# The second layer of an MLP as seven products of quarter sums for eight

## The reference

```python
def sq_relu_mlp(h, w1, w2):
    return jnp.square(jax.nn.relu(h @ w1)) @ w2
# in the layer:  x = x + gt2 * sq_relu_mlp(modulate(rms_norm(x, norm2), sh2, sc2), w_mlp1, w_mlp2)
```

## Time and profile before

| | |
|---|---|
| median of 3 runs | 1731.2 us (1731.02 to 1736.15) |
| profiled execution | 1733.65 us, its span 1731.8 us |
| TensorE busy | 1690.8 us, 98% |
| VectorE, ScalarE, GpSimd busy | 1010.1, 831.4 and 702.9 us (58%, 48%, 41%) |
| MLP stage | from 1376 us to the end |
| mean granted TensorE clock | 0.999 |

### The profile page before, as it was taken

One profiled execution on the slowest core, in us unless ns is written; L12 is line 12 of the kernel. 1 busy time (PEld: TensorE's weight loads), 2 busy tenths in 40 slices (PEclk: granted clock), 3 DMA queues, 4 the chain that ended last, 5 costly groups with the idle time before them and its releaser, 6 DMA issues.

```text
span 1731.8 us, 24615 instructions
## 1 busy us (share of the span) xinstructions
PE 1690.8 (98%) x8729; PEld 1381.5 (80%) x8729; DVE 1010.1 (58%) x1568; ACT 831.4 (48%) x1464; POOL 702.9 (41%) x795
## 2 busy tenths in 40 slices
PE   8999999989999999999999999999999999999998
PEld 6878787768686667878888888888888888888887
DVE  5578785697457755376668657787534533222222
ACT  4465665776366654366642454565423331313131
POOL 2634445426451024411124332323245465655554
PEclk9999999999999999999999999999999999999999
DMA  7362624223321002211058521112233233333333
GB/s 223 112 184 86 188 90 122 87 84 87 87 90 39 13 25 76 62 35 28 25 188 269 150 61 38 50 42 57 61 97 90 81 86 97 98 97 97 97 98 109
DMA packets 217149, 160.54 MB, mean 93 GB/s; under 512 B 8333, under 2 KB 190614, under 8 KB 217046
## 3 DMA queue, kind: packets, MB, share of 16 engines
q1 hardware_dynamic: 201758, 125.50, 25.3%
q10 hardware_dynamic: 15288, 33.66, 5.8%
HBM read 156.98 MB, written 2.16 MB: 92 GB/s over the span
## 4 chain that ended last, share of the span: by engine, by line
PE 77%; DVE 7%; ACT 6%; issue 5%; POOL 2%; DMA 1%; ACTq 0%; DVEq 0%; SPq 0%; POOLq 0%
PE ps L666 17%; PE ps L670 17%; PE ps L667 17%; PE ps L3226 3%; PE ps L3229 3%; PE ps L3227 3%; PE ps L2276 2%; POOL wl L616 2%; DVE mod_late L2672 2%; PE ps L2258 2%; PE ps L1683 1%; PE ps L2265 1%; PE ps L2822 1%; DMA ada_late<-w_ada 1%; ACT wh L629 1%
## 5 line engine op out<-in xcount | busy, mean ns | idle before, releaser
L616 POOL TENSOR_TENSOR wl<-raw,wh 128x256 fp32r<-128x256 f32 (+1 forms) x775 | 679.9, 907 | 967.8 <-ACT wh L629 967.8
L666 PE MATMUL ps<-ah,wh 128*128 128x512 f32 (+1 forms) x1144 | 457.4, 400 | 5.1 <-DVE al L794 2.2
L670 PE MATMUL ps<-ah,wl 128*128 128x512 f32 (+1 forms) x1144 | 447.3, 391 | 0.2
L667 PE MATMUL ps<-al,wh 128*128 128x512 f32 (+1 forms) x1144 | 446.3, 390 | 0.0
L629 ACT ACTIVATE wh<-raw 128x1024 fp32r<-128x1024 f32 (+1 forms) x220 | 230.7, 1049 | 300.2 <-PE ps L670 141.7
L666 PEld LDWEIGHTS ps<-ah,wh 128*128 128x128 f32 (+1 forms) x1144 | 214.0, 187 | 58.2 <-issue 7.2
L670 PEld LDWEIGHTS ps<-ah,wl 128*128 128x128 f32 (+1 forms) x1144 | 213.7, 187 | 49.3 <-POOL wl L616 1.9
L667 PEld LDWEIGHTS ps<-al,wh 128*128 128x128 f32 (+1 forms) x1144 | 214.2, 187 | 44.0 <-issue 1.7
L666 PE MATMUL ps<-bh,wh 128*128 128x512 f32 (+1 forms) x332 | 133.3, 402 | 0.7 <-DVE bl L1518 0.5
L670 PE MATMUL ps<-bh,wl 128*128 128x512 f32 (+1 forms) x332 | 129.6, 390 | 0.1
L667 PE MATMUL ps<-bl,wh 128*128 128x512 f32 (+1 forms) x332 | 129.5, 390 | 0.0
(11 more groups left out here) (468 smaller groups left out, 2938.4 us busy)
## 6 DMA issues: line engine op xcount, KB each, us to landing
raw<-w_mlp SPq DMA_DIRECT2D x64, 512.0 KB, 3.9
raw<-w_in SPq DMA_DIRECT2D x52, 512.0 KB, 3.8
raw<-ssm_w_in SPq DMA_DIRECT2D x40, 512.0 KB, 4.1
ada_late<-w_ada ACTq DMA_DIRECT2D x16, 1024.0 KB, 7.9
ada_raw<-w_ada ACTq DMA_DIRECT2D x16, 512.0 KB, 4.7
cum_rows<-cum_saved ACTq DMA_DIRECT2D x16, 512.0 KB, 3.9
raw<-ssm_w_out SPq DMA_DIRECT2D x16, 512.0 KB, 3.3
raw<-mla_w_in SPq DMA_DIRECT2D x11, 512.0 KB, 4.0
```

The lines of the kernel that those rows point to most:

```text
L616: nc.gpsimd.tensor_tensor(wl[:, s, part], raw[:, s, part], wh[:, s, part].bitcast(F32), ALU.subtract).then_inc(lo_ready, LOW_PIECES * (par ...
L666: nc.tensor.matmul(dst, w_hi[k], x_hi[k], start=k == 0, stop=False)
L667: nc.tensor.matmul(dst, w_hi[k], x_lo[k], start=False, stop=False)
L670: ins = nc.tensor.matmul(dst, w_lo[k], x_hi[k], start=False, stop=k == n - 1)
```

## The change

The second layer is done as one level of Strassen's scheme (Winograd's form). The 1024 hidden columns of a trip and the 512 tokens are cut into halves, the weights of the trip (1024 x 1024) into four quarters of 512 x 512. Seven products of sums of quarters replace eight products of quarters.

- **Layout.** `hidden(n)` sends even units to chunks 0 to 3 and odd ones to chunks 4 to 7, so that units 2m and 2m + 1 hold the four pieces (128 x 256) that are summed.
- **Token sums.** After each odd unit VectorE forms four sums of 128 x 256 (`hidden_sums`); ScalarE makes high parts (`sums_high`) and VectorE low parts (`sums_low`).
- **Weights.** The second layer's weights no longer pass through `raw`. ScalarE's queue loads four quarters of 1 MB per trip (`load_quarter`). VectorE forms differences in place (`quarter_sum`, 1024 columns an operation), ScalarE makes high parts (`mid_high`), VectorE the low parts of five products (`mid_low`), GpSimd of two (P3 and P2), in pieces of 512 columns.
- **Products.** TensorE takes them in the order P1, P5, P6, P3, P7, P2, P4, each 24 matmuls: two halves of the weights, two token tiles, two chunks, three parts. Products that feed the same output follow each other into one bank where the scheme allows. P1 waits for all low parts but the last.
- **Output.** VectorE adds the banks to an accumulator `acc` over all four trips; the gate is applied once, in the last trip.

```diff
-        ("mlp", 4, [full] * 16),
+        ("mlp", 4, [full] * 8),
...
+        MID = ("P1", "P5", "P6", "P3", "P7", "P2", "P4")
+        MID_BANKS = ((2, 3), (4, 5), (2, 3), (4, 5), (2, 3), (6, 7), (2, 3))
+        MID_SIDE = (3, 5)
...
 # TensorE
+            def product(i, r):
+                first, goes_on = isinstance(i, int) and i == 0, r not in MID_BEGINS
+                for u in range(2):
+                    vh, vl = mid_slot(r, u)
+                    pe.wait_ge(*again("mid_high", i, MID_UNITS, mid_unit(r, u)))
+                    if MID[r] in ("P1", "P2") and u == 0:
+                        pe.wait_ge(sem("hid_low"), i * DC + DC - (MID[r] == "P1") + AHEAD)
+                    elif MID[r] == "P5":
+                        pe.wait_ge(*again("sums_low", i, DC // 2, MID_KS * (u + 1)))
+                    for t in range(2):
+                        dst = bank(MID_BANKS[r][t])
+                        if u == 0 and (MID_FORMER[r] >= 0 or not first):
+                            pe.wait_ge(sem("o_free"), i * MID_UNITS + 2 * MID_FORMER[r] + t + 1)
+                        for n in range(MID_KS):
...
 # ScalarE, trip i
+                load_quarter(i, 0)
                 for n in range(DC + 1):
...
-                        split_ahead(act, "mlp", i, n)
+                        if n < DC - 2:
+                            split_ahead(act, "mlp", i, n)
+                        else:
+                            mid_high(i, 1, n - DC + 2)
...
+                        if n % 2 == 0:
+                            sums_high(i, n // 2 - 1)
+                    if n in (0, 2, 4):
+                        load_quarter(i, (1, 3, 2)[n // 2])
+                    if n == 3:
+                        for u in range(2):
+                            mid_high(i, 0, u)
+                for r in range(2, len(MID)):
+                    for u in range(2):
+                        mid_high(i, r, u)
...
 # VectorE
+            def hidden_sums(i, m):
+                early, late = norm_v[:, 2 * m % 3], norm_v[:, (2 * m + 1) % 3]
+                a11, a21, a12, a22 = early[:, 0:HALF], early[:, HALF:T], late[:, 0:HALF], late[:, HALF:T]
...
+                nc.vector.tensor_tensor(sums[:, S1], a21, a22, ALU.add).then_inc(ready, 1)
+                nc.vector.tensor_tensor(sums[:, S3], a11, a21, ALU.subtract).then_inc(ready, 1)
...
+                nc.vector.tensor_tensor(sums[:, S2], sums[:, S1], a11, ALU.subtract).then_inc(ready, 1)
...
+                nc.vector.tensor_tensor(sums[:, S4], a12, sums[:, S2], ALU.subtract).then_inc(ready, 1)
+            def sums_low(i, m):
+                dve.wait_ge(*again("sums_high", i, DC // 2, m + 1))
+                nc.vector.tensor_tensor(sum_lo[:, :, m], sums[:, 0:3], sum_hi[:, :, m].bitcast(F32), ALU.subtract)
+                nc.vector.tensor_tensor(bl[:, m, HALF:T], sums[:, S3], bh[:, m, HALF:T].bitcast(F32),
+                                        ALU.subtract).then_inc(counts("sums_low"), 1)
...
 # VectorE, trip i, n = 0 to 8, after the square of n
+                        if n % 2:
+                            hidden_sums(i, n // 2)
                     if n:
+                        c, tok = hidden(n - 1), slice(0, HALF if n % 2 else T)
                         dve.wait_ge(sem("hid_high"), i * DC + n)
...
+                        if n % 2 == 0:
+                            sums_low(i, n // 2 - 1)
...
+                    if n == 3:
+                        for u in range(2):
+                            mid_low(i, 0, u)
+                    elif n == 4:
+                        landed(i, 1)
+                        for u in range(2):
+                            quarter_sum(i, 0, u, 0, 1, 0)
+                    elif n == 5:
+                        landed(i, 3)
+                        for u in range(2):
+                            quarter_sum(i, 1, u, 1, 3, None)
+                    elif n == 6:
+                        mid_low(i, 1, 0)
+                        quarter_sum(i, 2, 0, 0, 3, 1)
+                    elif n == 7:
+                        mid_low(i, 1, 1)
+                quarter_sum(i, 2, 1, 0, 3, 1)
+                taking(0, 0)
+                taking(0, 1)
...
 # GpSimd, after the eight units of a trip
+                        for r, u in side_lows:
+                            pool.wait_ge(*again("mid_high", i, MID_UNITS, mid_unit(r, u)))
...
+                            for n in range(MID_KS):
+                                ins_ = nc.gpsimd.tensor_tensor(lo[:, n], src[:, n], hi[:, n].bitcast(F32), ALU.subtract)
```

More of the change, by code:

```diff
@@ L51 @@
 LATE_COLS = 16
-OUT_KS = 2
+MID_KS = 2
+hidden = lambda n: n // 2 + DC // 2 * (n % 2)
 K_UNIT = KVH + 1
@@ L461, in unit_source @@
                 return w_out2[:, :, bass.ds(i * 256 + n * P, P)]
[L462 to L465, removed]
+            return mlp1[:, :, bass.ds(i * 1024 + hidden(n) * P, P)]
         HEAD_STAGES = ("mla_kv", "mla_q")
@@ L3212, in pe_end @@
             stay_busy(1, 10)
[L3213 to L3232, removed]
@@ L3257, in block @@
                     project(bank(n % 2), "mlp", n, chunk(ah), chunk(al), DC, P, low=low).then_inc(unit_done, 1)
[L3258 to L3267, removed]
+                if first:
+                    pe.wait_ge(sem("out_copied"), 9)
+                for r in range(len(MID)):
+                    product(i, r)
             mlp_blocks(pe, block)
@@ new lines, in block @@
+                    if n in (0, 2, 4):
[6 more added lines that the diff above has]
+                        mid_high(i, r, u)
+                if not (isinstance(i, int) and i):
+                    for n in range(DC - 2, DC):
+                        act.wait_ge(*again("mid_done", i, MID_UNITS, mid_unit(5, n - DC + 2)))
@@ new lines, in quarter_of, with take @@
+            def quarter_of(r, t):
+                rows, cols = MID_QUARTER[r]
+                return 2 * rows + t, slice(cols * T, (cols + 1) * T)
+            def take(i, r, t):
+                tile, cols = quarter_of(r, t)
+                dst, src = acc[:, tile, cols], bank(MID_BANKS[r][t])
+                product_ready(i, r, t)
+                if isinstance(i, int) and i == 0 and MID_QUARTER[r] not in MID_QUARTER[:r]:
+                    nc.vector.tensor_copy(dst, src).then_inc(sem("o_free"), 1)
+                    return
+                former = [q for q in range(r) if MID_QUARTER[q] == MID_QUARTER[r]]
+                dve.wait_ge(sem("o_free"), i * MID_UNITS + (2 * former[-1] + t + 1 if former else 0))
+                nc.vector.tensor_tensor(dst, dst, src, ALU.add).then_inc(sem("o_free"), 1)
@@ L3338, in block @@
             def block(i):
+                last = isinstance(i, int) and i > 0
+                taking = lambda r, t: (last_take if last and (r, t) in FINAL else take)(i, r, t)
                 for n in range(DC + 1):
@@ new lines, in block @@
+                quarter_sum(i, 2, 1, 0, 3, 1)
+                taking(0, 0)
+                taking(0, 1)
+                landed(i, 2)
+                for u in range(2):
+                    mid_low(i, 2, u)
+                    quarter_sum(i, 3, u, 0, 2, 2)
+                if last:
+                    for t in range(2):
+                        tile, cols = quarter_of(6, t)
+                        st(gated_add(t, acc[:, tile, cols], cols, tile))
+                        st.wait()
+                taking(1, 0)
```

180 lines of the change are left out of this document (160 added, 20 removed).

## The result

The changed kernel took 1754.7 us (median of 4 runs, 1753.0 to 1756.3) against 1733.3 for the kernel before (4 runs, 1731.0 to 1736.2, the three above and one more): ratio 1.0125 [1.0112, 1.0137], 21.5 us slower. The forecast was +13.5, 1745, with a range to 1759; the measured loss is 8 us larger than forecast. The profiled execution took 1753.04 us, span 1751.2, mean granted clock 0.989.

A forecast was written before the change was run, and what follows sets the result against it. TensorE, busy 98% of the span, was taken to bound the kernel. Removed unit -21.8, stalls +28.9 and clock +6.4 give +13.5 us on the median of 1731.2: 1744.7, rounded to 1745, range 1732 to 1759.

The forecast's parts named there:

- The removed unit: Second layer on TensorE: one unit of 24 matmuls fewer per trip, 4 x 5.44 = 21.8 us less.
- The stall ahead of P1: TensorE waits before P1 for VectorE's low part of chunk 6: 7.6 + 3 x 7.1 = 28.9 us.
- Latency of 3.7: Wait from unit 7's end to chunk 6's low part even if VectorE is never late: 3.7 us.
- the conflict: GpSimd bursts slow VectorE on shared SBUF ports in iterations 3 to 5: 1.6 us each, 4.9 in all.
- 2.1 us behind at U(7): VectorE's lateness at the first matmul behind unit 7, from 23.0 us of work in 21.76, without other loss.
- rival C: Port conflict in full between U(3) and U(7): P1 at U(7) + 10.6, +27.5 us, 1759; chance 0.12.
- The clock: TensorE's clock falls after each stall ahead of P1: 1.6 us each, 6.4 in all.
- Rival D: The forecast stall, with the clock down for all of P1: 7.1 + 4 x 4.8 = +26, 1757; chance 0.10.
- The rest, costed at nothing: Products, takes, loads and end after P1 starts: covered, 0 us; P3's banks tight, worth perhaps 1 us.
- Rival B: Wait ahead of P1 is only data latency, 3.7 to 4.7 us per trip, clock holds: 1724 to 1729; chance 0.11.
- A: The forecast itself: VectorE late at U(7), stall of 6 to 8 us per trip, clock falls; +4 to +19; chance 0.60.
- E: Late VectorE takes in the last trip or a held raw load: +2 to +6 on A; chance 0.07.

The follow-up runs named there:

- experiment 4: Changed kernel with VectorE's weight work moved out of iterations 3 to 7, P1's single wait kept; 1744.6 us, ratio 1.0070.
- experiment 2: Changed kernel with GpSimd's low parts of the first layer's weights cut from 256 to 8 columns a piece in the MLP stage; 1745.0 us, ratio 1.0077.
- Experiment 1: Changed kernel with 28 matmuls of 512 columns that feed nothing put ahead of P1's wait; 1748.1 us, ratio 1.0093.
- experiment 6: Changed kernel with the last trip's gate and add of P4's quarter moved to iteration 0; 1750.9 us, ratio 1.0107.
- experiment 7: Changed kernel with the edits of experiment 5 and experiment 6, P6's differences and lows reordered, residual copies awaited only where needed; 1722.2 us, ratio 0.9946.
- experiment 3: Changed kernel with P1 waiting for each chunk's low part separately, 18 of its 24 matmuls ahead of chunk 6; 1737.4 us, ratio 1.0030.
- experiment 5: Changed kernel with both P1's wait for each chunk and VectorE's weight work moved out of iterations 3 to 7; 1728.7 us, ratio 0.9982.

## Why the prediction was right or wrong

**The removed unit, -21.8: right.** The first layer takes 43.57 us (43.52 before) and there are 24 matmuls fewer in each trip.

**The stall ahead of P1, +28.9: right, as a sum and in its parts.** Forecast 7.6 and 3 times 7.1, measured 7.34, 7.29, 7.29 and 6.96; that the two sums agree to the tenth is luck, since misses on either side cancel. Latency of 3.7: shown by experiment 4 (3.8 to 4.0). Lower bound of 4.7 without the conflict: shown by experiment 2 (4.68). Charged at 4.9, the conflict counted for 7.1 - 4.7 = 2.4 in the stall, since without it VectorE waits for ScalarE instead; taking it away gave 7.29 - 4.68 = 2.6. The iterations came as 7.1, 7.0, 5.9, 5.1 and 3.0 against 6.7, 6.6, 6.7, 5.0 and 2.8: the fifth paid less of it, the third and fourth more. One reading on the way was wrong: 23.0 us of work in 21.8 do not make VectorE 2.1 us behind at U(7). Of the 23.0, 2.8 belong to iteration 7, which can't begin before its own unit ends; iterations 3 to 6 are 20.2 us in 21.8, so without conflict and waits VectorE is on time, and 2.1 lies below the 3.7 of latency. The sum of 7.0 is sound all the same, since with 4.9 of conflict iteration 7 begins at U(7) + 4.2, which is what the trace shows. A stall of 10.6 (rival C) did not happen. The lock rule of the Trainium skill (SBUF — State Buffer, section "SBUF: two separate sides") has the direction right, as experiment 2 shows. What was too high is the price that rival C made of it, the full length of each burst, 8.5 us for three. Beside the three bursts of trip 1 VectorE's rows grew by 1.9, 2.0 and 0.7 us in iterations 3, 4 and 5, 4.6 in all, where the forecast charged 4.9. A burst is four pieces of 0.7 us, and single rows beside it grew by at most 0.54, which a lock held for one piece at a time allows.

**The clock, 4 x 1.6 = +6.4: too small.** The granted clock fell in all four stalls and cost 2.8, 2.8, 2.8 and 1.4: 9.8 us. The size was taken from the one low stretch of the kernel before, which lasted 3.4 us. Here it lasted 10.2 us in three trips and 6.8 in the last, and 5.9 (2.9 in the last) of it lay over P1. Rival D (all of P1 at the lower level, 4.8) stood on the other side. Experiment 1 shows the price by itself.

**The rest, costed at nothing: wrong by 4.8 us.** Three pieces. P3's wait in the last trip, 2.2 us, was named in the walk of the queue as "perhaps 1 us" and left out of the sum; experiment 6 takes it away. The forecast's own list of signs had "no other idle over 1 us in the stage", and said that it is wrong "if P5 to P4 have stalls": by these words this wait counts against it. The products' pitch is 0.229 us, 38.5 for 168, where the forecast carried 0.2267 over: 0.4 in each trip, 1.7. Nothing tried here says why; in trip 0 of experiment 7 the second halves of P5, P3 and P2 keep 0.227, and all other halves stand at 0.229 to 0.231, but for two late matmuls in P7. And the end is 5.64 us from the last matmul's start to the end of the span, where it was 4.76: 0.9. VectorE's last product with the gate begins 1.8 us behind that matmul, before it was 0.9: its queue, not the store, is what grew.

Together -21.8 + 28.9 + 9.8 + 2.2 + 1.7 + 0.9 = +21.7; from the stage's first matmul to the end of the span the traces show 355.8 before and 377.8 after, +22.0. The two spans differ by 19.4 only, since the stage begins 2.6 us earlier after (1373.4 for 1376.0): the changed kernel's trace lacks the fall of the clock of the earlier trace rows, and 2.3 of the 2.6 arise between 930 and 1010 us, around it. The medians differ by 21.5.

Rival B (latency only) is refuted by the stalls. A holds as a mechanism, but the measured +21.5 lies 2.5 us past its +4 to +19. E, the late takes, is true as an addition to A; it had 0.07.

## What to carry to other kernels

Where one engine is busy without a pause, work taken from it is worth its full time only if the first consumer behind the cut does not need the newest output of the layer before. Walk the supplying engine's queue iteration by iteration, with the bursts of its neighbour, let no iteration begin before its own input is there, and price the last element it must deliver; then give the consumer a wait for each piece, in the order in which the pieces come. Neither that nor a levelled queue alone made this change pay; both together brought it level (0.2% faster), and the other moves of experiment 7, the gate's among them, made it 0.5% faster. A stall here cost a third more of itself in clock (9.8 on 28.9).

## What was not expected of the hardware

- The clock fell behind idles of 3.8 to 7.3 us (from matmul start to matmul start less one pitch) each time, 17 of 17 in the traces of the kernel after and experiments 2, 3, 4 and 6, and stayed at the lower level while the matmuls ran again: 5.9 us of them in trip 0 of the kernel after. Below that the length of the idle alone does not decide (here the waits as the profile counts them): the same 2.9 us in experiment 3 was followed by a fall in trip 1 and by none in trip 2, 1.9 us in experiment 1 by a fall in trip 0, and the 2.2 us ahead of P3 by none in the kernel after and by one in experiment 2.
- The forecast took the idle of 2.53 us near 371 for one that the clock holds through. It stands in all ten traces, in a stage that no edit touches, and in five of them (experiments 1, 2, 4, 5 and 6) the clock fell behind it for 3.4 us; in experiment 1:
```profile
373.50:376.00 2.50, 2.34 (x14) 0.51 0.02 7
```
The low stretch near 976 is in four (before, experiments 3, 4 and 5). The MLP stage begins at 1373.4 to 1373.6 us where neither came, at 1375.0 to 1376.0 where one did and at 1376.7 to 1376.9 where both did. So one trace shows what the clock did once, and up to 3.5 us between two executions arise ahead of the MLP stage, and the change and the experiments touch only that stage.
- VectorE's step from one of its operations to the next that waits for it costs the 0.1 us of the forecast where the wait is direct: in trip 1, iteration 7, independent sums start 0.34 us apart and the last one, which needs the one before it, 0.45. Behind the square it costs 0.39 (the rows with DVEq): there VectorE first waits for the square, then raises a second semaphore, and then waits for that one.
- The conflict of VectorE and GpSimd takes from both: 0.42 to 0.96 for 256 columns, 0.69 to 1.78 for 512, and 1.3 to 2.2 and more for a low part of 512 on GpSimd.
